# Branch D's head projections interleaved with the big column blocks, values last, in a two-layer four-branch transformer trunk

## The reference

```python
aq, ak, av, bq, bk, bv, cq, ck, cv, dqa, dckv, dkr, gates = _split_in(h @ p['w_in'])
aq = pos(_rms(aq.reshape(B, T, A_HEADS, 2, A_QK), p['a_qk_g'][0]))     # bq, bk, cq, ck likewise
dq = (_rms(dqa, p['d_qnorm_g']) @ p['w_d_qb']).reshape(B, T, D_HEADS, D_QK)
dq = _rms(dq, p['d_qk_g'][0])
kv = (ckv @ w_kvb).reshape(B, L, D_HEADS, D_NOPE + D_V)                # ckv: _rms(dckv), and the cache
k = jnp.concatenate([kv[..., :D_NOPE], jnp.broadcast_to(kr[:, :, None, :], (B, L, D_HEADS, D_ROPE))], axis=-1)
kd, vd = _rms(k, kn_g), kv[..., D_NOPE:]
```

## Time and profile before

| | us |
|---|---|
| median of 3 runs | 5363.93 (5355.14 to 5369.72) |
| the profiled execution | 5360.51 |
| its span in the profile | 5358.7 |
| projections up to the values, layer 0 / 1 | 156.2 / 134.2 |
| Branch D's stage, layer 0 / 1 | 80.0 / 86.7 |

### The profile page before, as it was taken

How to read it: one execution, slowest core, us unless ns; L and a number is a source line. 1 busy time by engine, 2 the same in 40 slices (tenths; PEclk the granted TensorE clock), 3 DMA queues, 4 the chain that set the end, 5 groups by cost and what they waited for, 6 DMA issues and landing times.

```text
span 5358.7 us, 68340 instructions
## 1 busy us (share of the span) xinstructions
PE 5084.0 (95%) x25512; PEld 4122.9 (77%) x25512; DVE 3207.9 (60%) x7231; ACT 1677.1 (31%) x2610; POOL 1328.6 (25%) x860
## 2 busy tenths in 40 slices
PE   7889999889999999999989899998899999999999
PEld 4746787678888887888866467878788888788887
DVE  3575311128998876666655752111498998666666
ACT  3234321223333332222232343212233333322222
POOL 3200121314334421111132001213244344211111
PEclk8979999999999999999999799999999999999999
DMA  7100121455787788888811001222467877888886
GB/s 261 61 10 1 35 73 61 152 202 195 273 271 240 255 294 305 291 291 289 287 67 51 10 1 45 69 64 63 148 229 259 279 267 235 314 292 291 289 290 221
DMA packets 349128, 981.98 MB, mean 183 GB/s; under 512 B 31648, under 2 KB 100128, under 8 KB 345504
## 3 DMA queue, kind: packets, MB, share of 16 engines
q1 hardware_dynamic: 215232, 553.19, 31.8%
q0 software_dynamic: 74880, 276.86, 14.8%
q10 hardware_dynamic: 58720, 148.04, 7.1%
HBM read 829.43 MB, written 148.54 MB: 183 GB/s over the span
## 4 chain that ended last, share of the span: by engine, by line
PE 85%; DVE 6%; ACT 2%; DMA 2%; issue 1%; POOL 1%; DVEq 1%; ACTq 0%; SPq 0%; POOLq 0%
PE PS L868 26%; PE PS L828 23%; PE PS L496 15%; PE PS L485 5%; PE PS L850 4%; PE PS L630 3%; PE PS L656 2%; PE PS L486 1%; PE PS L640 1%; DVE AR L1249 1%; POOL HR L1593 1%; PE PS L600 1%; PE PS L816 1%; DVE SM L1288 1%; DMA gates_by_expert<-AR 1%
## 5 line engine op out<-in xcount | busy, mean ns | idle before, releaser
L868 PE MATMUL PS<-HB,VR 128*128 128x512 f32 x6144 | 1396.6, 390 | 18.0 <-DVE HB L1550 18.0
L868 PEld LDWEIGHTS PS<-HB,VR 128*128 128x128 f32 x6144 | 1155.5, 188 | 259.1 <-issue 18.8
L828 PE MATMUL PS<-HR,UR 128*128 128x512 f32 x4128 | 1013.2, 399 | 0.0
L1593 POOL TENSOR_TENSOR UR<-WR,UR 128x1024 fp32r<-128x1024 f32 x212 | 528.7, 2494 | 1792.2 <-ACT UR L1061 938.0
L496 PE MATMUL PS<-HR,UR 128*128 128x320 f32 (+1 forms) x5952 | 924.1, 315 | 36.6 <-POOL HR L1593 34.8
L496 PEld LDWEIGHTS PS<-HR,UR 128*128 128x128 f32 x5952 | 889.2, 191 | 68.6 <-issue 47.1
L828 PEld LDWEIGHTS PS<-HR,UR 128*128 128x128 f32 x4128 | 768.2, 190 | 167.0
L1537 DVE TENSOR_TENSOR VR<-HT,VR 128x1024 fp32r<-128x1024 f32 x256 | 313.7, 1225 | 459.0 <-ACT VR L1179 390.0
L1179 ACT CAST VR<-HT 128x1024 fp32r<-128x1024 f32 x256 | 268.8, 1050 | 961.2 <-PE PS L868 958.7
L828 PE MATMUL PS<-HR 128*128 128x512 f32 x2016 | 486.7, 394 | 0.0
L828 PEld LDWEIGHTS PS<-HR 128*128 128x128 f32 x2016 | 372.1, 188 | 73.6
(11 more groups left out here) (193 smaller groups left out, 5961.3 us busy)
## 6 DMA issues: line engine op xcount, KB each, us to landing
WR<-in_uT SPq DMA_DIRECT2D x256, 512.0 KB
HT<-in_vtab SPq DMA_DIRECT2D x256, 512.0 KB, 3.9
activations<-AR ACTq DMA_DIRECT2D x256, 256.0 KB
gates_by_expert<-AR ACTq DMA_DIRECT2D x128, 512.0 KB, 3.5
HW<-activations SPq DMA_DIRECT2D x256, 256.0 KB
WR<-gates_by_expert SPq DMA_DIRECT2D x64, 1024.0 KB
AR<-in_ada SPq DMA_DIRECT2D x40, 1024.0 KB, 6.4
WR<-in_wgate SPq DMA_DIRECT2D x64, 640.0 KB, 3.8
```

The lines of the kernel that those rows point to most:

```text
L828: last = pe.matmul(bank(n % 2), u_part(n, w)[:, c, :], HR[:, h, c, 0:LAT], start=c == 0 and i == 0, stop=c == DC - 1 and i == 2)
L868: last = pe.matmul(bank(d), VR[:, m % 4, w, P * d:P * d + P], HB[:, (m + 1) % 3, h, :], start=m == 0 and i == 0, stop=m == E1 - 1 and i == 2)
L1593: nc.gpsimd.tensor_tensor(dst, src, high.bitcast(F32), ALU.subtract).then_inc(sem_, 1)
```

## The change

The list `items` starts with qa, ckv and kr, and each of the eight blocks from ak0 on is followed by one small item (dq and dk in turn): a pair. PE's order in a pair of block n and small item n + 1 is: three chunks of block n, the sums of the small item before, a rotation, five chunks of block n, another rotation, the small projection, the sums of block n. ACT's order in a pair is root, raw copy, high half of the block two ahead, root, raw copy. POOL's cosine products stand before and behind the low half. DVE keeps its order (norm of an item, then rope of the item before), now over the new list; its three instructions for the modulation of layer 0 come at item 13 instead of 9. `d_values` and the sums of dk3 follow the last pair, and the four value blocks come at the end of the phase, with the three last rotations between them; each value block takes its tiles in the order 3, 2, 4, 1, 0. Branch D's values are copied by ACT under the first value block, and the copy to VT is the last thing in the phase.

The small weights no longer use the ring: wdq (with the value part of wkv, 512 KB) goes to the unused columns of WR's four slots, loaded ahead of the wait for h; the key part (192 KB) goes to free memory of HT behind the caches. STD moves from VD's memory to VT's, and the staging of layer 0's modulation to that of QT, DK and VT. The semaphore counts follow, and the host packs the weights in the new order.

```diff
@@ items
-    items = ([("aq", 0), ("aq", 1), ("ak", 0), ("ak", 1), ("bq", 0), ("bq", 1), ("bk", 0), ("cq", 0), ("cq", 1),
-              ("ck", 0), ("qa", 0), ("qa", 1), ("ckv", 0), ("kr", 0)]
-             + [("dq", h) for h in range(HEADS)] + [("dk", h) for h in range(HEADS)])
+    items = [("qa", 0), ("qa", 1), ("ckv", 0), ("kr", 0), ("aq", 0), ("aq", 1), ("ak", 0), ("dq", 0), ("ak", 1), ("dk", 0),
+             ("bq", 0), ("dq", 1), ("bq", 1), ("dk", 1), ("bk", 0), ("dq", 2), ("cq", 0), ("dk", 2), ("cq", 1), ("dq", 3),
+             ("ck", 0), ("dk", 3)]
...
+    steps = [(n, n + 1 if n + 1 in small_no else None) for n in block_of]
@@ buffers
-        STD = VD.rearrange("p a b -> p (a b)").rearrange("p (a b) -> p a b", a=2)
+        STD = VT[:, 0:3, :].rearrange("p a b -> p (a b)").rearrange("p (a b) -> p a b", a=2)
+        WDQ = WR[:, :, D:D + 2 * D_QK].rearrange("p h (k d) -> p h k d", k=2)
+        WDV = WR[:, :, D + 2 * D_QK:SLOT]
+        WDK = HF[:, 8 * LAT + TOK:8 * LAT + TOK + HEADS * D_QK].rearrange("p (h d) -> p h d", h=HEADS)
@@ sync
+                sp.dma_start(WR[:, :, D:SLOT], wdq[l]).then_inc(d_in, 16)
                 sp.wait_ge(hr_ready, l * (2 * DC) + DC)
...
                 sp.dma_start(VT[:, 4, :], cache_v[l]).then_inc(l_in, 16)
+                sp.dma_start(WDK.rearrange("p h d -> p (h d)"), wkv[l]).then_inc(d_in, 16)
...
-                load(l, B_DQ, WR[:, B_DQ % RING, 0:2 * HEADS * D_QK], wdq[l])
-                load(l, B_KV, WR[:, B_KV % RING, 0:HEADS * (D_QK + HD)], wkv[l])
@@ tensor
+            VALUE_TILES = (3, 2, 4, 1, 0)
+
+            def values(l, n):
+                if n == 0:
+                    pe.wait_ge(y_ready, (l + 1) * NI)
+                pe.wait_ge(split, l * N_SPLIT + (SPLIT_NO[B_V + n] + 1))
+                w = UR[:, SPLIT_NO[B_V + n] % 2]
+                for t in VALUE_TILES:
+                    if n == 0 and t == 4:
+                        pe.wait_ge(dv_out, l + 1)
...
-                for s in range(NI + 2):
-                    if l == 0 and s < DC:
-                        rest_step(2 * s)
-                        rest_step(2 * s + 1)
-                    if l == 0 and s == 9:
-                        turn_rest()
-                    if s == N_FM:
-                        values(l)
-                    if s < NI:
...
-                        project(l, s)
-                    if 1 <= s <= NI:
-                        head_sums(l, s - 1)
-                    if s >= 2:
-                        rotate(l, s - 2)
+                for k, (n, small) in enumerate(steps):
+                    if l == 0 and k < DC:
+                        rest_step(2 * k)
+                        rest_step(2 * k + 1)
+                    if l == 0 and k == 9:
+                        turn_rest()
+                    project(l, n, 0, 3)
+                    if k >= 1:
+                        head_sums(l, n - 1)
+                    if n >= 3 and n - 1 in small_no and n - 3 in small_no:
+                        rotate(l, n - 3)
+                    if n >= 2 and n - 1 not in small_no:
+                        rotate(l, n - 2)
+                    project(l, n, 3)
+                    if n - 1 in small_no:
+                        rotate(l, n - 2)
+                    elif small is not None:
+                        rotate(l, n - 1)
+                    if small is not None:
...
+                        project(l, small)
+                        head_sums(l, n)
                 d_values(l)
+                head_sums(l, NI - 1)
+                values(l, 0)
+                rotate(l, NI - 3)
+                rotate(l, NI - 2)
+                values(l, 1)
+                rotate(l, NI - 1)
+                for n in range(2, N_V):
+                    values(l, n)
                 phase_end(pe, l, 1)
@@ scalar
-                for s in range(NI + 1):
...
-                    if s < N_FM:
-                        high(l, B_FM + s + 2)
...
-                    if s < NI:
-                        raw(l, s)
-                    if s >= 1:
-                        std(l, s - 1)
+                for k, (n, small) in enumerate(steps):
...
+                    if k >= 1:
+                        std(l, n - 1)
+                    raw(l, n)
+                    high(l, B_FM + k + 2)
+                    if small is not None:
+                        std(l, n)
+                        raw(l, small)
+                act.wait_ge(dv_ready, l + 1)
+                nc.scalar.copy(VD[:, 0:4, :].rearrange("p a b -> p (a b)"), PF[:, 0:1024])
+                nc.scalar.copy(VD[:, 4:6, :].rearrange("p a b -> p (a b)"), bank(7)).then_inc(dv_out, 1)
+                std(l, NI - 1)
...
                 act.wait_ge(yn_ready, (l + 1) * NN)
-                nc.scalar.copy(VD.rearrange("p a b -> p (a b)"), PF[:, 0:256 * KTILES])
+                for t in range(TILES):
+                    nc.scalar.copy(VT[:, t if t < 4 else 5, :], bank(t if t < 4 else 7))
@@ vector
-                    if l == 0 and s == 10:
+                    if l == 0 and s == 14:
@@ gpsimd
-                for s in range(NI + 2):
-                    if s < N_FM:
-                        low_block(l, B_FM + s + 2)
...
-                    if s - 2 in rope_no:
-                        cos_part(s - 2)
+                for k, (n, small) in enumerate(steps):
+                    if n - 1 in small_no:
+                        cos_part(n - 2)
+                    low_block(l, B_FM + k + 2)
+                    if n - 1 in rope_no:
+                        cos_part(n - 1)
+                cos_part(NI - 2)
+                low_block(l, B_V + 2)
+                cos_part(NI - 1)
+                low_block(l, B_V + 3)
```

More of the change, by code:

```diff
@@ L73, in loads @@
     first = N_FIRST if l else 0
-    pairs = 0 if l else sum(m % RING == n % RING for m in range(N_FIRST) if m < n)
-    before = loads(l - 1, BLOCKS + n % RING) if l else 0
-    return before + (n - first) // RING - (pairs if n % 2 else 0)
+    own = sum(m % RING == n % RING and m not in (B_DQ, B_KV) and (m >= N_FIRST or m % 2 == 0) for m in range(first, n))
+    return own + (loads(l - 1, BLOCKS + n % RING) if l else 0)
 def block_no(l, n):
@@ L306, in build @@
         v_out = sem("v_out")
+        d_in, dv_ready, dv_out = sem("latent_weights_in"), sem("latent_values"), sem("latent_values_out")
         st_out = sem("states_out")
@@ L534, in square_sums, with project @@
                     last.then_inc(ss_ready, 1)
[L536 removed]
+            def project(l, n, first=0, end=DC):
                 kind, j = items[n]
                 base = 1024 * (n % 2)
[L539 removed]
+                if n >= 2 and first == 0:
                     pe.wait_ge(y_ready, l * NI + (n - 1))
                 if kind == "dq":
[L542 removed]
                     if j == 0:
+                        pe.wait_ge(d_in, 32 * (l + 1))
                         pe.wait_ge(yn_ready, l * NN + (norm_no[at_item["qa", 1]] + 1))
[L545 removed]
                     for kc in range(2):
[L547 to L549 removed]
+                        last = both(cols(base, D_QK), WDQ[:, j, kc, :], lambda lo, hi: QA[:, kc, lo:hi], kc == 0, kc == 1)
+                    last.then_inc(pj_ready, 1)
                 elif kind == "dk":
[L551 to L552 removed]
+                    both(cols(base, D_QK), WDK[:, j, :], lambda lo, hi: KT[:, 4, lo:hi], True, False, KEYS)
                     both(cols(base, D_QK), sel_kr, lambda lo, hi: KR[0:D_ROPE, lo:hi], False, True, KEYS).then_inc(pj_ready, 1)
                 else:
[L555 to L556 removed]
+                    part = halves(l, B_FM + block_of[n])
+                    for c in range(first, end):
                         if n == 0:
@@ L560, in project @@
                         last = split_product(out, part, c, c == 0, c == DC - 1, of_h, spans)
-                    last.then_inc(w_used, 1)
+                    if end == DC:
+                        last.then_inc(w_used, 1)
             def head_sums(l, n):
@@ L588, in rotate @@
                 pe.matmul(bank(6, LAT, parts), m, YN[0:parts, r % 2, :], start=True, stop=True).then_inc(rot_ready, 1)
-            def values(l):
-                pe.wait_ge(y_ready, l * NI + N_FM)
-                pe.wait_ge(rest_kept, 1)
-                for n in range(N_V):
-                    pe.wait_ge(split, l * N_SPLIT + (SPLIT_NO[B_V + n] + 1))
-                    w = UR[:, SPLIT_NO[B_V + n] % 2]
-                    for t in range(TILES):
-                        for cc in range(2):
-                            c = 2 * n + cc
-                            for m, (h, x) in enumerate(((0, 0), (1, 0), (0, 1))):
-                                last = pe.matmul(bank(t if t < 4 else 7), HR[:, h, c, qcols(t)], w[:, x, cc * 512:(cc + 1) * 512],
-                                                 start=c == 0 and m == 0, stop=c == DC - 1 and m == 2)
-                    last.then_inc(w_used, 1)
@@ L604, in d_values @@
-            def d_values(l):
-                pe.wait_ge(y_ready, l * NI + NI)
```

(9 more changed lines are left out.)

63 lines of the change are left out of this document (25 added, 38 removed).

## The result

The changed kernel takes 5305.7 us at the median of 4 runs (5300.2 to 5320.3), the kernel before 5362.4 (5355.1 to 5369.7, 4 runs). The ratio is 0.9896 with a 95% interval of 0.9877 to 0.9915: 56.7 us less. The profiled execution of the changed kernel took 5300.2 us. The forecast was 5291 us, with a range of 5268 to 5322.

The account below looks back on a forecast made before the run. PE bounds the kernel (85% of the last-ending chain), but DVE paces Branch D's stage. Terms gave 38.8 us in layer 1 and 30.4 in layer 0, together 69.2: 5360.5 - 69.2 = 5291.3 us, range 5268 to 5322.

Parts of the forecast that it names:

- rival 1: In the pairs, POOL's low halves hold DVE's two-input instructions; 5305 to 5318 us, middle 5312; chance 18%.
- (b): Tail: rotations of dq3 and ck back to back after the first value block; the second waits for DVE, 1.5 us.
- (a): Stage head: aq1's rotation stands behind only five eighths of the next block after its sums; 4.3 us lost in each layer.
- (e): SP's queue: dq and dk weight loads stand in front of block 4 and two modulation blocks; 1 us lost, layer 0.
- (d): Layer 0: three small DVE modulation instructions move to the sixth pair, where DVE binds; 2.5 us lost.
- Branch D's own stage goes: Branch D's separate stage is removed, PE's remaining work for it kept; gains of 40.1 us in layer 0, 46.8 in layer 1.
- What DVE takes back in the pairs: DVE needs 14.8 us a pair, 1.3 more than PE; five of eight pairs bind, 6.5 us lost a layer.
- (c): Two earlier PE waits, behind rotations and before the kr block, fall away or are covered; 4.3 us gained a layer.
- At nothing: Effects put at 0: DVE's last norms and value-block halves covered by values, the moved copies, and attention's possible clock gain.
- Rival 2: DVE does not bind in the pairs; their excess and two rotation waits vanish, about 5274 us; chance 12%.
- rival 3: PE's clock falls in the pairs, slower than before; 5490 us if at the lower level throughout; chance 4%.
- rival 4: The waits only move, PE idling 5.4 us in each pair; no change, 5360 us; chance 4%.

Follow-up runs that it names:

- e9: On the changed kernel with both rotation moves (dq3's and aq1's): reciprocals of the ten roped-block items leave out their last 256 of 640 columns; 5289.0 us in one run.
- e2: On the changed kernel: aq1's rotation is issued in the next pair, behind dq0's sums, instead of in front of dq0's projection; 5303.7 us (0.9876).
- e1: On the changed kernel: dq3's rotation is issued ahead of the first value block instead of behind it; 5301.6 us (0.9866).
- e7: On the changed kernel: POOL makes dk3's cosine product before the low half of the third value block; 5327.8 us in one run.
- e6: On the changed kernel with dq3's and aq1's rotations moved: all three last rotations stand ahead of the first value block; 5326.9 us (0.9919).
- e5: On the changed kernel with dq3's and aq1's rotations moved: reciprocals of Branch D's eight small items leave out their last 256 columns; 5293.4 us (0.9857).
- e4: On the changed kernel: items keep their new places, but PE and ACT take them one after the other in the old order; 5400.3 us (1.0063).

## Why the prediction was right

The likeliest case came, inside the range, for the reason given: DVE sets the pace of the pairs, and the clock stays at 1.00. The total alone doesn't tell it from rival 1, whose 5305 to 5318 us hold the measured 5305.7; the rows do. Of the signs named, the stages of 216.9 and 238.5 us (about 213 and 236 forecast), DVE busy 95% in the pairs, waits of about 1 us there and the clock came. "Nothing waits between value blocks" did not.

The miss of 14.4 us (5291.3 against 5305.7) has three parts: 69.2 - 63.6 = 5.6 us in the stages, 63.6 - 60.3 = 3.3 elsewhere in the span, and 5.5 because the profiled execution of the changed kernel is that much under its median. By the rows, (b) adds 4.3 us in layer 1, where the stage was 3.9 over the sum. In layer 0, 1.7 over it, (b) adds 3.2 and (a) and (e) 0.5 each; (d) gives some 1.8 back and the pairs 0.5. Step by step:

- *Branch D's own stage goes* (40.1 and 46.8). Right in kind. The 46.8 rested on one execution of 86.7 us; the second took 80.1, which makes it 40.2. One profile of a stage that waits isn't its length.
- *What DVE takes back in the pairs* (6.5 us a layer). Right in cause and sum, with luck in the sum. A pair takes 15.0 us against 14.8 forecast; the eight waits in the pairs of layer 0 sum to 6.0 us, the nine of layer 1 to 6.7. But PE needs 13.9, not 13.5, so a pair costs 1.1 us and not 1.3, and in layer 1 the waits begin with the third pair (0.48 us), so six pairs bind at 1.1, not five at 1.3. e9 shows that it is DVE's durations that count.
- *(a), the head* (4.3). Right mechanism. The rows give 2.57 us of wait and 1.7 of slow small products in layer 1, 2.99 and 1.8 in layer 0. The slow part doesn't come in each execution, and e2's stages give 2.8 to 5.8 us.
- *(b), the tail* (1.5). This term was mis-sized: "two DVE instructions, of which the sum is 0.69 us at the median". It cost about 4.7 us in layer 0 (3.38 of wait, 8.59 instead of 7.3 for the block) and 5.8 in layer 1. I had named the cause, as rival 1, but looked for it in the pairs and not here, where no reciprocal covers the low half. e1 shows the size (5.5 and 5.1 to 8.0 us a layer), e7 the cause.
- *(c)* As said; neither of the two waits of the earlier trace rows is left.
- *(d), the rest of the modulation* (2.5). Too high: the three instructions took 0.23, 0.23 and 0.18 us, and PE's wait in that pair was 1.31 us instead of 0.60. The 2.38 us of the earlier trace rows were POOL's hold, and it no longer met them.
- *(e), the loads* (1). PE waited 2.92, 0.57 and 0.87 us for modulation blocks, 1.5 us more than the two waits of before.
- *(f)* Not isolated by any run.
- *At nothing.* The cover by the values held, and e6 prices it at 14 us a layer. Whether attention gained from the denser work ahead of it can't be told: in layer 1 it took 257.5 us after 257.4 in the first profiles and 269.3 after 272.2 in the second.
- *Rival 1* was real at the tail of each layer and, with the cosine products instead of the low halves, in the pairs (1.06 us for 0.69); the reciprocal covered the rest, as e5 showed by uncovering it. Not all of DVE's products are exposed, as the prediction had it: the sine product, with one input in PSUM, kept 0.69 us. *Rival 2* fell (DVE has no gaps), *rival 3* too (clock 1.00), and *rival 4* too, but e4 shows that it was near: with the plain order the waits don't only move, they cost more than before.

## What to carry to other kernels

Filling a bound engine's gaps with small work pays only if each engine's queue is ordered by when an operand is ready: the same interleaving gained 57 us with one order and lost 32 with the other. When two instructions of one chain are issued back to back, look at what runs beside the second engine at that moment, not at its median duration, and price the slow spell that can follow the wait along with it. Before cutting work on an engine, look at what that work covers: 1.6 us less in a small item's reciprocal was given back in whole or in part (1.9 and 0.6 us), where it uncovered a meeting with POOL; as much less in a block's reciprocal paid 1.1 us a pair, all that PE had waited.

## What was not expected of the hardware

- A DVE sum that meets POOL's products ends 0.55 us behind the last of them, however many follow each other: 0.69 us became 1.05 beside a cosine product, 2.44 beside a low half and 5.67 beside a cosine product and two low halves in a row. At the head of layer 0 the sum began first (140.28, the low half 140.47 us): there the sum took 0.69 and the low half 2.70 us instead of 2.35.
- The cost of a wait on PE can be more than the wait. In the changed kernel and the experiments, blocks behind waits of 3.4 to 6.0 us took 0.5 to 2.5 us more (8.59 and 9.72 for 7.3; 8.9 to 9.6 for 7.6; 6.51 for 5.0). Behind waits of 2.0 to 3.1 us it depended on the place and the execution: the first wait of layer 1's stage (2.57 and 2.56 us) had slow products behind it in the first profile of the changed kernel and none in the second. In the pairs, none was slower behind a wait of 1.3 us or less.
- The same stretch of the same kernel, with the same work on DVE, took 80.1 and 86.7 us in two executions, at a granted clock of 0.77 and 0.69, and attention 257 and 272 us. What decides it is open.
